# A two-layer SSD and HGRN2 encoder trunk on one core: where and how the SSD step sizes are computed

## The reference

```python
def rmsnorm(x, w):
    xf = x.astype(jnp.float32)
    xf = xf * lax.rsqrt(jnp.mean(xf * xf, axis=-1, keepdims=True) + NORM_EPS)
    return (xf * w.astype(jnp.float32)).astype(x.dtype)
...
def ssd_mixer(z, xbc_raw, dt_raw, conv_w, conv_b, dt_bias, a_log, d_skip, norm_w):
    ...
    dt = jax.nn.softplus(dt_raw + dt_bias)
    A = -jnp.exp(a_log).reshape(SSD_GROUPS, R)
    ...
    x_dt = xs * dt[..., None]
    a_cum = jnp.cumsum(dt * A, axis=2)
    ...
    decay_end = jnp.exp(a_cum[:, :, -1:] - a_cum)
    contrib = jnp.einsum('bcsgn,bcsgr,bcsgrp->bcgrpn', Bm, decay_end, x_dt)
    ...
for l in range(DEPTH):                                    # DEPTH = 2
    x = x + 0.5 * swiglu(rmsnorm(x, ffn1_norm[l]), ffn1_w_gate[l], ffn1_w_up[l], ffn1_w_down[l])
    h = rmsnorm(x, mix_norm[l])
    proj = (h @ w_in[l]).astype(f32)
    z, xbc, dt_raw, q_raw, f_raw, i_raw, g_raw = jnp.split(proj, split_idx, axis=-1)
    y_ssd = ssd_mixer(z, xbc, dt_raw, ...)
    y_hg = hgrn2_mixer(q_raw, f_raw, i_raw, g_raw, lower_bounds[l], ...)
    x = x + jnp.concatenate([y_ssd, y_hg], axis=-1) @ w_out[l]
    x = x + 0.5 * swiglu(rmsnorm(x, ffn2_norm[l]), ffn2_w_gate[l], ffn2_w_up[l], ffn2_w_down[l])
return rmsnorm(x, final_norm)
```

## Time and profile before

| | |
|---|---|
| median of three runs | 2000.38 us (2000.17 to 2002.25) |
| the profiled execution | 1997.81 us |
| its span, first to last instruction | 1996.1 us |
| PE busy | 1966.8 us, 99% |
| PEld, the loading of weights into PE | 1618.8 us |
| DVE, ACT, POOL busy | 789.1, 691.5, 836.4 us |
| mean granted clock of PE | 0.993 |
| chain that ended last | PE 90%, DVE 6%, issue 2%, ACT 1% |

### The profile page before, as it was taken

The page is one execution under the profiler, slowest core; times in us unless marked ns, Lnnn a source line. Parts: engine busy times, 40 slices in busy tenths (PEclk is TensorE's granted clock), DMA queues, the critical chain, the costliest instruction groups (busy, mean ns, idle before and its releaser), DMA issues.

```text
span 1996.1 us, 28972 instructions
## 1 busy us (share of the span) xinstructions
PE 1966.8 (99%) x10604; PEld 1618.8 (81%) x10604; DVE 789.1 (40%) x1225; ACT 691.5 (35%) x953; POOL 836.4 (42%) x358
## 2 busy tenths in 40 slices
PE   8999999998999999999999999999999999999998
PEld 6888888887778888888888888888778788888887
DVE  6222221487786422211132222116878763222112
ACT  5232222454433322222332322236444333222222
POOL 3444445442223544444444444444422235444443
PEclk9999999999999999999999999999999999999999
DMA  5322233221112322233323223332211123222332
GB/s 181 96 97 102 89 98 98 90 81 54 55 63 85 104 96 95 95 96 97 104 85 102 95 98 88 98 98 85 76 55 63 43 95 116 95 95 92 98 96 94
DMA packets 54855, 181.65 MB, mean 91 GB/s; under 512 B 8432, under 2 KB 8432, under 8 KB 54768
## 3 DMA queue, kind: packets, MB, share of 16 engines
q1 hardware_dynamic: 54208, 180.44, 28.3%
q10 hardware_dynamic: 560, 0.07, 0.0%
HBM read 178.40 MB, written 2.10 MB: 90 GB/s over the span
## 4 chain that ended last, share of the span: by engine, by line
PE 90%; DVE 6%; issue 2%; ACT 1%; DMA 0%; DVEq 0%; ACTq 0%; SPq 0%
PE ps L1337 28%; PE ps L1339 28%; PE ps L1338 28%; PE ps L1460 1%; PE ps L1459 1%; PE ps L1458 1%; DVE xs L982 1%; PE ps L1352 1%; ACT th L536 0%; DVE w L1046 0%; PE ps L1518 0%; ACT e L536 0%; DVE g L935 0%; PE ps L1567 0%; DVE g L929 0%
## 5 line engine op out<-in xcount | busy, mean ns | idle before, releaser
L450 POOL TENSOR_TENSOR wlo<-raw,whi 128x1024 fp32r<-128x1024 f32 x344 | 834.1, 2426 | 1148.9 <-ACT whi L496 591.3
L1337 PE MATMUL ps<-hhi,whi 128*128 128x512 f32 x1776 | 700.1, 394 | 14.1 <-DVE hs L1085 6.4
L1339 PE MATMUL ps<-hhi,wlo 128*128 128x512 f32 x1776 | 694.6, 391 | 0.0
L1338 PE MATMUL ps<-hlo,whi 128*128 128x512 f32 x1776 | 694.3, 391 | 0.0
L1337 PEld LDWEIGHTS ps<-hhi,whi 128*128 128x128 f32 x1776 | 335.2, 189 | 90.9 <-issue 13.9
L1339 PEld LDWEIGHTS ps<-hhi,wlo 128*128 128x128 f32 x1776 | 335.3, 189 | 70.9
L1338 PEld LDWEIGHTS ps<-hlo,whi 128*128 128x128 f32 x1776 | 335.4, 189 | 67.8
L496 ACT ACTIVATE whi<-raw 128x1024 fp32r<-128x1024 f32 x168 | 177.3, 1055 | 306.7 <-PE ps L1339 287.1
L1337 PE MATMUL ps<-ahi,whi 128*128 128x512 f32 x704 | 273.9, 389 | 0.0
L1338 PE MATMUL ps<-alo,whi 128*128 128x512 f32 x704 | 273.9, 389 | 0.0
L1339 PE MATMUL ps<-ahi,wlo 128*128 128x512 f32 x704 | 273.9, 389 | 0.0
(11 more groups left out here) (239 smaller groups left out, 1455.9 us busy)
## 6 DMA issues: line engine op xcount, KB each, us to landing
raw<-in_up SPq DMA_DIRECT2D x168, 512.0 KB, 3.3
raw<-in_mix SPq DMA_DIRECT2D x66, 512.0 KB, 3.3
raw<-in_dn SPq DMA_DIRECT2D x64, 448.0 KB, 3.3
raw<-in_dn SPq DMA_DIRECT2D x32, 512.0 KB, 3.5
raw<-in_lead SPq DMA_DIRECT2D x8, 512.0 KB, 3.2
x<-in_x SPq DMA_DIRECT2D x8, 256.0 KB, 5.8
raw<-in_lead SPq DMA_DIRECT2D x8, 256.0 KB, 6.0
out<-stage SPq DMA_DIRECT2D x4, 512.0 KB, 3.5
```

The lines of the kernel that those rows point to most:

```text
L450: pool.tensor_tensor(wlo[:, q, :], raw[:, q, :], whi[:, q, :].bitcast(F32), ALU.subtract).then_inc(split.sem, 1)
L1337: mm(dst, whi[:, q, s], mh, start=start, stop=False)
L1338: mm(dst, whi[:, q, s], ml, start=False, stop=False)
L1339: return mm(dst, wlo[:, q, s], mh, start=False, stop=stop)
```

## The change

The block of `dt` leaves `PROJ`, and `C` is loaded in two halves as `B` is, so that the number of weight blocks stays. The 8 weight columns of each of the 8 feature tiles (32 KB) are loaded to `dtw` by a DMA of their own, multiplied by the norm's gain on DVE, and put into `wg`, 32 columns wide with 24 zeros. After the block of `f0`, PE makes eight fp32 matmuls of 512 columns straight from `x`, in four groups of 32 output partitions (`dt_products`). ACT copies the 128x512 result, PE adds the four groups with `sel` and turns it (`dt_select`, after `f1`), and softplus and the product with `A` run with tokens on partitions as 128x32 instructions. The running sum is one fp32 product with a triangle of ones (`dt_cumulate`, after `q0`); the value at the tile's end follows after the first block of values, and the turning back of the sums after the second (`sums_turn`). `rsqrt` keeps its intermediate values in PSUM and no longer splits its result; `spread` is four fp32 matmuls instead of eight fp32r ones. In the `z` steps DVE makes `xde` and `xdt` before the gate of `z`.

```diff
 PROJ = ([("f", 0), ("f", 1), ("f", 2), ("f", 3), ("q", 0)]
-        + [("q", 1), ("B", 0), ("q", 2), ("C", 0), ("dt", 0), ("q", 3), ("g", 0)]
+        + [("q", 1), ("B", 0), ("q", 2), ("C", 0), ("q", 3), ("g", 0)]
...
-    PBLOCKS += [(_n, 0, 4), (_n, 4, 8)] if _kind == "B" else [(_n, 0, 8)]
+    PBLOCKS += [(_n, 0, 4), (_n, 4, 8)] if _kind in ("B", "C") else [(_n, 0, 8)]
...
+        wg = place("wg", [P, KD, 32], 10)
+        dtq = place("dtq", [P, T], 8)
+        ahl = place("ahl", [P, TC, 40], 11, F32R)
...
+                sp.wait_ge(dt_w.sem, dt_w.upto(l, 0))
+                sp.dma_start(dtw[:], dt_in[l + 1]).then_inc(dtw_in.sem, 16)
...                                                        # ScalarE
                 for n, (kind, pr) in enumerate(PROJ):
                     keep_up(n)
+                    if n == AT["f", 1]:
+                        ready(dt_raw)
+                        do(dt_copied, dtq[:], bank(7), ACT.Copy)
...
+                    if n == AT["f", 2]:
+                        ready(dt_abs)
+                        do(dt_exp, wend[:], wend[:], ACT.Exp)
...
+                    if n == AT["f", 3]:
+                        ready(dt_exp)
+                        do(dt_log, wend[:], wend[:], ACT.Ln, bias=1.0)
...
+                        hi(VALUES0 + 1 + NS)
+                        ready(to_end)
+                        do(to_end_exp, wend[:], wend[:], ACT.Exp)
+                        ready(acb_turned)
+                        do(acb_split, acbs[:], bank(3)[0:40, :], ACT.Copy)
...
-                    if kind == "dt":
-                        ready(dt_abs)
-                        do(dt_exp, acb[:], acb[:], ACT.Exp)
-                        ready(dt_exp)
-                        do(dt_log, acb[:], acb[:], ACT.Ln, bias=1.0)
...                                                        # VectorE
-            def rsqrt(e, rms, parts, src, scale):
+            def rsqrt(e, rms, bk, at, n, scale):
-                n, dst = src.shape[1], rms[:]
-                ms, tmp = ntn[:, 0, 0:n], ntn[:, 1, 0:n]
-                did(ts(ms, src, scale, EPS, ALU.mult, ALU.add))
+                src, minus_half, tmp = (bank(bk)[:, at + i * n:at + i * n + n] for i in range(3))
+                did(ts(minus_half, src, -0.5 * scale, -0.5 * EPS, ALU.mult, ALU.add))
...
-                if parts is None:
-                    return
-                settle()
-                did(dve.tensor_copy(parts[:, 0, :], dst))
-                settle()
-                tt(parts[:, 1, :], dst, parts[:, 0, :].bitcast(F32), ALU.subtract).then_inc(e.sem, 1)
...
+                did(dve.memset(wg[:].rearrange("p k m -> p (k m)"), 0.0))
+                did(dve.memset(ahl[:].bitcast(F32).rearrange("p c m -> p (c m)"), 0.0))
+                settle()
+                dve.wait_ge(dtw_in.sem, dtw_in.upto(l, 15))
+                made(dt_w, tt(wg[:, :, 0:8], dtw[:], par[:, WN:WN + KD].unsqueeze(2).to_broadcast([P, KD, 8]),
+                              ALU.mult))
                 norm(l, 1)
...
                 def dt_first():
-                    ready(proj_out, AT["dt", 0])
-                    did(ts(dtb[:], dtb[:], par[0:8, DTB:DTB + 1], None, ALU.add))
+                    ready(dt_tokens)
+                    did(tt(dts[:, 0], in_heads(0), rt[:].unsqueeze(2).to_broadcast([P, TC, 8]), ALU.mult))
                     settle()
-                    made(dt_abs, stt(acb[:], dtb[:], -1.0, dtb[:], ALU.mult, ALU.min))
+                    did(tt(dts[:, 0], dts[:, 0], each_tile(par[:, DTB:DTB + 8]), ALU.add))
+                    settle()
+                    made(dt_abs, stt(wend[:], dts[:, 0], -1.0, dts[:, 0], ALU.mult, ALU.min))
                 def dt_rest():
                     ready(dt_log)
-                    did(stt(dtb[:], dtb[:], 0.0, acb[:], ALU.max, ALU.add))
+                    did(stt(dts[:, 0], dts[:, 0], 0.0, wend[:], ALU.max, ALU.add))
                     settle()
-                    did(ts(acb[:], dtb[:], par[0:8, NEGA:NEGA + 1], None, ALU.mult))
-                    settle()
-                    for c in range(TC):
-                        a = acb[:, c * P:(c + 1) * P]
-                        ins = dve.tensor_tensor_scan(a, ones[0:8, 0:1].to_broadcast([8, P]), a, 0.0, ALU.mult, ALU.add)
-                        ...
+                    made(dt_made, tt(dts[:, 1], dts[:, 0], each_tile(par[:, NEGA:NEGA + 8]), ALU.mult))
+                def dt_out():
+                    ready(dt_sums)
+                    did(dve.tensor_copy(dts[:, 1], in_heads(1)))
+                    did(dve.tensor_copy(ahl[:, :, 0:8], in_heads(1)))
+                    settle()
+                    made(dt_tok, tt(ahl[:, :, 32:40], in_heads(1), ahl[:, :, 0:8].bitcast(F32), ALU.subtract))
...
+                    if n == AT["f", 2]:
+                        dt_first()
                     if n == AT["f", 3]:
                         hg_dist(0)
                         gate_key(0)
                         gate_key(1)
                         log_gate(2)
                         log_gate(3)
+                        dt_rest()
                         gate_key(2)
                         gate_key(3)
                     if n == AT["q", 0]:
                         evac(n)
+                        dt_out()
                         hg_k(0)
                         hg_tables()
                         settle()
                         key_levels(0)
+                        ends()
...
                     if kind == "z":
                         ready(proj_out, n)
+                        if pr == 0:
+                            end_weights()
+                        ssd_inputs(pr)
                         silu(("z", pr), g2[:, 0, :], zs[:, pr % 2, :])
...                                                        # TensorE
-            def spread(e, dst, parts):
+            def spread(e, dst, rms):
                 for c in range(TC):
-                    for part in range(2):
-                        last = mm(dst[:, c * P:(c + 1) * P], parts[:, part, c:c + 1].to_broadcast([P, P]), identr[:],
-                                  start=part == 0, stop=part == 1)
+                    last = mm(dst[:, c * P:(c + 1) * P], rms[:, c:c + 1].to_broadcast([P, P]), ident[:],
+                              start=True, stop=True)
...
-                def dt_turn():
-                    for a, src in enumerate((dtb, acb)):
-                        ...
+                def dt_products():
+                    ready(dt_w)
+                    for k in range(KD):
+                        g = 32 * (k % 4)
+                        last = mm(bank(7)[g:g + 32, :], wg[:, k, :], x[:, k, :], start=k < 4, stop=k >= 4)
+                    last.then_inc(dt_raw.sem, 1)
+                def dt_select():
+                    ready(dt_copied)
+                    for c in range(TC):
+                        last = mm(bank(3)[:, c * 8:c * 8 + 8], dtq[:, cols_of(c)], sel[:], start=True, stop=True)
+                    last.then_inc(dt_tokens.sem, 1)
+                def dt_cumulate():
+                    ready(dt_made)
+                    mm(bank(3)[:, TC * 8:2 * TC * 8], causal[:], dts[:, 1].rearrange("p c h -> p (c h)"),
+                       start=True, stop=True).then_inc(dt_sums.sem, 1)
...
+                def sums_turn():
+                    ready(to_end)
+                    for c in range(TC):
+                        last = mm(bank(3)[0:40, cols_of(c)], ahl[:, c, :].bitcast(F32), ident[:], start=True, stop=True)
+                    last.then_inc(acb_turned.sem, 1)
...
                     if n < 0:
                         values(k0 // 2, w)
+                        if k0 == 0:
+                            chunk_ends()
+                        if k0 == 2:
+                            sums_turn()
...
+                    if n == AT["f", 0]:
+                        dt_products()
+                    if n == AT["f", 1]:
+                        dt_select()
+                    if n == AT["q", 0]:
+                        dt_cumulate()
...
-                    if n == AT["g", 0]:
-                        dt_turn()
```

More of the change, by code:

```diff
@@ L30 @@
 BIG = 8e37
[L31 removed]
+MAGIC = float(0x5F3759DF - 2 ** 22 - 2 ** 30)
 NS = 4
@@ L1090, in hg_states @@
                             made(state, ins)
-                def dt_out():
-                    ready(dt_turned)
-                    made(dt_tok, dve.tensor_copy(dts[:].rearrange("p a c h -> p (a c h)"),
-                                                 bank(4)[:, 0:2 * TC * 8]))
                 def cb_mask():
@@ L1247, in _ @@
                         hg_k(2 if kind == "B" else 3)
-                    if kind == "dt":
-                        dt_first()
                     if n == AT["g", 0]:
@@ L1357, in norm_spreads @@
                 pe.wait_ge(norm_rms.sem, norm_rms.upto(l, ph))
-                spread(norm_spread, bank(NORM), rt2)
+                spread(norm_spread, bank(NORM), rt)
             def h_tile(k):
@@ L1824 @@
```

(2 more changed lines are left out.)

154 lines of the change are left out of this document (67 added, 87 removed).

## The result

The changed kernel takes 2011.51 us (median of 5 runs, 2010.44 to 2012.65), the kernel before 2000.17 us beside it (5 runs, 1996.04 to 2002.25). The ratio on record, which is not the quotient of these two medians (1.0057), is 1.0063, 95% interval 1.0051 to 1.0075: 0.6% slower. The profiled execution took 2011.51 us with a span of 2009.8, 13.7 us more than the span of before.

What follows compares the result with a forecast made beforehand. PE was taken as the bound. Per layer, work 4.3, waits 1.9 and 8.8, clock 1.7 twice, less 8.9 removed: +9.5; two layers less 0.4 give +18.6, 2019 us. Own range 2008 to 2028; 8 in 10, 2002 to 2030.

Steps and rivals of the forecast that it cites:

- The long wait: At dt_cumulate, end of q0, PE waits for DVE's dt_rest behind log_gate(3): 8.8 us a layer, bounds 3.7 and 11.
- the short one: At dt_select, after f1, PE waits for ACT's copy behind its hi: 1.9 us a layer, bounds 0 and 2.5.
- the waits for `rt` and `xde`: PE's waits at the norm's spread and the SSD inputs, claimed removed: 1.55 and 1.3 us a layer.
- The products: dt_products, 16 fp32 records in four groups running abreast: 2.1 us a layer, ends 0.9 and 8.5.
- The small terms: Added PE work: dt_select 0.9 us, dt_cumulate 0.2, sums_turn 1.1 a layer.
- the clock: Lower clock on PE behind each of the two new waits: 1.7 us each a layer, bounds 0 and 2.1.
- the small `acb` wait: PE's wait for the sums of dt, 0.4 us once, taken to show DVE and ACT relief off PE's path.
- the block's 5.45: Block of dt removed from PE: 24 matmuls at 0.227 us each, 5.45 us a layer.
- `hs` of the third pair: Before the end of g0, could be late; held covered, PE 5.45 us sooner, DVE and ACT some 7; else 1 us.
- `xde` and the turning: Removed from PE: the wait for xde, 1.3 us, and the turning of dtb and acb, 0.59 us, a layer.
- Rivals two and three: Wait at dt_cumulate absent or almost so, 1994.6 us, chance 0.13; or 3.7 us without clock falls, 2002.0 us, chance 0.10.
- the three steps: Lower end of own range, 2008: long wait 2 us shorter, dt_products 0.9, one fall of the clock less.

Runs made afterwards that it cites:

- Experiment 1: Kernel before, with only one wait added: PE waits at the end of q0 until DVE has done log_gate(3); 2019.22 us, ratio 1.0093.
- experiment 7: Changed kernel with the running sum two value blocks later and dt_out directly behind the first key products, ACT's copy left in place; 1991.16 us, ratio 0.9967.
- experiment 6: Changed kernel with the running sum two value blocks later, dt_out behind the first key products, and ACT's copy ahead of its other work; 1980.93 us, ratio 0.9921.
- experiment 5: Kernel before, with only the changed norm factors and ssd_inputs moved ahead of the z gate, dt as before; 1990.25 us, ratio 0.9961.
- Experiment 4: Changed kernel with all eight fp32 products of 512 columns in one group of 32 output partitions; 2022.23 us, ratio 1.0114.
- experiment 3: Changed kernel with only ACT's copy of the dt products moved ahead of its rounding of the next weights in f1; 2008.34 us, ratio 1.0044.
- Experiment 8: Changed kernel with 38 unread fp32 products of 128x128 on PE in front of its wait for dts; 2010.58 us, ratio 1.0068.
- Experiment 9: Kernel before, with ten unread fp32 products of 128x128 on PE directly before its wait for hs in block C; 2002.95 us, ratio 1.0015.

## Why the prediction came out as it did

**Right, with the mechanism.** Slower, by a new wait at `dt_cumulate` for `dts` and a shorter one at `dt_select` for `dtq`, on top of a change whose work is a gain. The long wait was worked out at 8.8 us and is 8.97; the short one at 1.9 and is 1.63. Experiment 1 shows the long one to be enough by itself. Taking the long one away (experiment 7) turns the changed kernel's ratio of 1.0063 into 0.9967, and both (experiment 6) into 0.9921, and the waits for `rt` and `xde` give back what they were (experiment 5). The time, 2011.5, lies in the range; 2019 is 7.5 us too high, and that it is not further off is in part luck, since terms of several us missed in both directions, as shown below.

**The products.** Forecast 2.1 us at the value of four abreast, measured 379.24 - 377.38 = 1.86. Experiment 4 puts the sequence at 7.05, inside the forecast's end of 8.5. The Trainium skill (TensorEngine Tiling (Array Packing), Tiling Modes and Theoretical Speedup) has up to four times for 128x32 tiles; the trace has 3.7 times and shows no drain worth pricing at the change of mode: the next product starts 0.06 us before the modelled end of the group.

**The small terms.** `dt_select` was put at 0.9 and takes 388.92 - 387.55 = 1.37 in layer 0; `dt_cumulate` at 0.2 and takes 417.68 - 417.23 = 0.45. These two ran at the lower clock: experiment 3, without the wait, has 385.91 - 385.10 = 0.81 for the first, and experiment 6 shows the sum's two records at full clock in 0.30 us from first start to last end, instead of 0.63. They were priced from rows at full clock although they stand directly behind a wait. In layer 1 `dt_select` takes 0.92.

**The mis-sized term, first part: the clock.** Forecast 1.7 us behind each wait. Behind the long one a product takes 0.42 us instead of 0.227 for 4.3 us, so half of 4.3, some 2.2, were lost. Behind the short one the clock was 0.54 over 6.7 us in layer 0, which loses 0.46 x 6.7 = 3.1 us and lies beyond the forecast's bound of 2.1, and 0.69 over 5.5 us in layer 1, which loses 1.7. So the losses on PE are as forecast or larger, and up to `C` they are in the delay. Whether they can all be added to the run time is less sure. In experiment 1 the cost over the waits themselves, 4.5 us (1.7 to 7.5), is about what the low clock takes. Experiment 8 took the loss behind the long wait away and the run did not get faster by a measurable amount, where 4.4 us were expected; its interval (1.0050 to 1.0086) does not exclude 2 us.

**Second part, and the larger one: what the removed dt chain had hidden.** The prediction costed the relief of DVE and ACT after `C` at nothing, since it is off PE's path, "as the small `acb` wait shows". The small wait showed the opposite: at the end of `g0` PE and the dt chain were level to within 0.4 us, so PE's own stalls ahead of it cost nothing there, and could be won only together with the chain. Experiment 9 removes them alone and gets a wait of 4.67 us. The changed kernel removes the chain, its wait for `hs` happens to be short, and the stage to `g0` shrinks by 9.4 and 8.9 us in the two layers, not by the block's 5.45: 7.4 us in all beyond the forecast. Against that stands one thing that the prediction held to be covered, at 1 us if not: `hs` of the third pair, for which PE now waits 1.81 us at the end of `g0` in each layer.

**The sum, by place.** Against +19.0 without the `acb` wait, and with the spans' +13.7 as measured. Up to the last product of `C` the forecast per layer was 18.4 - 1.55 = 16.9; measured are 20.1 in layer 0 and (1471.36 - 1444.10) - 9.5 = 17.8 in layer 1, together 4.1 too much: the small terms, the clock, and 0.5 us by which the norm's product of layer 0 already starts later (374.30 against 373.80). From there to `g0`, 7.4 more was given back. Behind it the forecast was -1.9 a layer (`xde` and the turning); measured are 9.5 - 10.7 = -1.2, and, in layer 1, 4.2 - 17.8 + 8.9 = -4.7, together 2.1 more given back. 19.0 + 4.1 - 7.4 - 2.1 = 13.6. The medians are 2.4 us closer together than the spans, since the profiled run of before (1997.81) was 2.4 us under its median.

**Rivals two and three** gave the second wait 0 to 3.7 us. It is 8.97: instructions ran long beside POOL's subtraction again, though not the same ones. The scan in the step of `f2` took 3.30 us (3.31 before), the bound 2.20 (1.46), the scan of `log_gate(2)` 3.25 (1.23), and the difference that had taken 2.83 took 0.66. For the bound the prediction took 0.67, another instruction's time, as the free value; its like takes 0.40 in both traces, so that its lower end of 3.7 should have been 3.4. And the three steps that it names for its lower end, 2008, give 2019 - 4 - 2.4 - 3.4 = 2009.

**Open.** Why the gaps without a releaser inside the scores move: 1.9 us behind `C` before, 1.1 and 0.8 us ahead of it after, none of 1.9 in experiment 9. Why `hs` is waited for 0.97 us and not 3.2 follows from these gaps lying ahead of it, but not from where they come. Layer 1 costs 4.2 us and layer 0 9.5 under the same program, and the traces show where: 1.8 us of the difference arise up to `C`'s last product, where the clock behind the short wait is low for longer in layer 0, and 3.7 behind `g0`, where it falls at the head sums in layer 0 only. Why it falls in one layer and not in the other, after the same wait or the same products, was not tested. Nor is it known why the waits for `hs` grow when the early copy is left out of experiment 6's kernel.

## What to carry to other kernels

Before a product is placed on the engine that bounds the kernel, find the instruction that makes its operand and what stands ahead of it in its own queue: here 0.4 us of VectorE work behind a gate chain cost 9 us per layer. Taking the product two blocks of values later, with VectorE's next step behind the first key products, and ScalarE's copy to the front made a loss of 0.6% a gain of 0.8%. A short wait of the bounding engine on another says that the two are level there, not that the other has slack: stalls ahead of it are free until that chain goes, and are won with it. A loss of clock read behind a wait need not be a cost: where another engine sets a later start, filling the wait with work moves the idle time there, and in experiments 8 and 9 the low clock with it.

## What the runs showed of the hardware

- Fp32 products with 512 columns and 32 output columns: 0.44 us a record in one group, 16 records in 1.86 us in four.
- After 9 us of idle time the granted clock was 0.50 over the next 4.3 us; with the same time filled by products of 128x128 nobody reads, the products behind it ran at their full pace. After 3.2 us idle it was 0.60 over 4.3 us, after 0.96 or 0.97 us it stayed at 1.00.
- After the same wait the clock did not always do the same. Behind 1.56 us idle (`rt`) it was 1.00 over 5.5 us in the kernel before and 0.69 in experiment 9; behind 1.63 us (`dtq`) 0.54 over 6.7 us in layer 0 of the changed kernel, 0.69 over 5.5 us in layer 1, and 1.00 over 5.9 us in layer 0 of experiment 7.
- It fell without a wait at 32 records with 8 columns: 0.81 over 9.2 us in both layers before, 0.63 and 1.00 in the two layers after.
- A VectorE difference of 128x512 took 2.64 us instead of 0.69 while GpSimd subtracted 128x1024, two subtractions in 5.16 us against 2.40 for one alone.
- Gaps of 0.5 to 1.9 us without a releaser occur within runs of some hundred small products, and move from one stage to another when products elsewhere are moved.
